# Three conditioning chunks of a two-block transformer kernel computed elsewhere: two in the convolution stage and QKV instead of at the ends of two feed-forward stages

## The reference

```
x = x + rms_norm(mixer(rms_norm(x)))            # block 1: stick-breaking attention, pooling, gating
x = x + rms_norm(relu(h @ w_ff_in)**2 @ w_ff_out)
for i in 0, 1:                                  # block 2: layer 0 conformer convolution, layer 1 attention
    mod = silu(c) @ ada_w[i] + ada_b[i]         # one row of 6 * 1024
    sh1, sc1, g1, sh2, sc2, g2 = split(mod, 6)
    h = rms_norm(x) * (1 + sc1) + sh1
    x = x + g1 * (conv(h) if i == 0 else attention(h))
    h = rms_norm(x) * (1 + sc2) + sh2
    x = x + g2 * (relu(h @ mlp_w1[i])**2 @ mlp_w2[i])
```

## The kernel before, in words

| chunks | where |
|---|---|
| 0, 1 | QKV of block 1 |
| 2, 3 to 8, 9 | first feed-forward stage (`mlp_*` with m = 0): head, loop of three, tail (`ADA_TAIL`) |
| 10 | its end (`ADA_LAST`): first half before the last unit's split, second half after, the sum between the last two units of TensorE, the keeping ahead of what VectorE does to the stage's result |
| 11, 12 | convolution (`ADA_MID`); loaded by GpSimd (`mid_load`, line 854) |
| 13, 14 to 19, 20, 21 | second feed-forward stage (m = 1), as the first |
| 22, 23 | third feed-forward stage (m = 2) |

## Time and profile before

### The profile page before, as it was taken

The page is one execution under the profiler, slowest core; times in us unless marked ns, Lnnn a source line. Parts: engine busy times, 40 slices in busy tenths (PEclk is TensorE's granted clock), DMA queues, the critical chain, the costliest instruction groups (busy, mean ns, idle before and its releaser), DMA issues.

```text
span 1094.3 us, 16806 instructions
## 1 busy us (share of the span) xinstructions
PE 1047.4 (96%) x6872; PEld 922.7 (84%) x6872; DVE 704.1 (64%) x829; ACT 492.0 (45%) x554; POOL 109.7 (10%) x76
## 2 busy tenths in 40 slices
PE   6999998999999999998899999999997799999998
PEld 6997777899999998985689999998886489999996
DVE  4868656687666778653578666687574648454463
ACT  5346446444444445331454443445444844444441
POOL 0030001001001002023101000100000401100000
PEclk9999999899999999998999999999999899999999
DMA  8884435728878783796229787874554224555540
GB/s 291 304 303 132 143 116 159 288 81 310 293 253 290 272 280 105 216 260 197 79 77 345 254 288 265 283 264 145 192 193 133 98 78 154 193 184 199 185 162 39
DMA packets 118716, 221.58 MB, mean 202 GB/s; under 512 B 6338, under 2 KB 20740, under 8 KB 118660
## 3 DMA queue, kind: packets, MB, share of 16 engines
q1 hardware_dynamic: 116944, 214.97, 58.0%
q0 software_dynamic: 1520, 5.77, 1.6%
q10 hardware_dynamic: 196, 0.05, 0.0%
HBM read 215.07 MB, written 1.05 MB: 197 GB/s over the span
## 4 chain that ended last, share of the span: by engine, by line
PE 82%; DVE 8%; ACT 5%; issue 3%; DMA 2%; SPq 1%; ACTq 0%; DVEq 0%
PE ps L410 76%; ACT hi L348 2%; PE ps L870 2%; DVE lo L359 1%; PE ps L447 1%; DVE ada_acc L893 1%; DMA ada_raw<-in_ada_w 1%; PE ps L724 1%; PE ps L650 1%; DVE stat L1914 1%; DMA raw<-in_w_in 0%; DVE hTl L497 0%; ACT aS L1617 0%; DVE aS L1909 0%; ACT gate L1518 0%
## 5 line engine op out<-in xcount | busy, mean ns | idle before, releaser
L359 DVE TENSOR_TENSOR lo<-raw,hi 128x2048 fp32r<-128x2048 f32 x153 | 355.9, 2332 | 277.7 <-ACT hi L348 276.9
L348 ACT ACTIVATE hi<-raw 128x2048 fp32r<-128x2048 f32 x153 | 292.4, 1913 | 332.5 <-PE ps L410 318.8
L410 PE MATMUL ps<-hTh,hi 128*128 128x256 f32 x992 | 282.7, 285 | 2.0 <-DVE hTl L497 1.9
L410 PE MATMUL ps<-hTh,lo 128*128 128x256 f32 x992 | 280.7, 283 | 0.0
L410 PE MATMUL ps<-hTl,hi 128*128 128x256 f32 x992 | 280.6, 283 | 0.0
L410 PEld LDWEIGHTS ps<-hTh,hi 128*128 128x128 f32 x992 | 190.2, 192 | 3.8 <-DVE hTl L497 2.5
L410 PEld LDWEIGHTS ps<-hTl,hi 128*128 128x128 f32 x992 | 190.3, 192 | 0.3
L410 PEld LDWEIGHTS ps<-hTh,lo 128*128 128x128 f32 x992 | 190.3, 192 | 0.0
L410 PE MATMUL ps<-hi,hidh 128*128 128x512 f32 x416 | 162.9, 392 | 0.4 <-DVEq L645 0.4
L410 PE MATMUL ps<-hi,hidl 128*128 128x512 f32 x416 | 162.1, 390 | 0.0
L410 PE MATMUL ps<-lo,hidh 128*128 128x512 f32 x416 | 162.0, 389 | 0.0
(11 more groups left out here) (219 smaller groups left out, 877.6 us busy)
## 6 DMA issues: line engine op xcount, KB each, us to landing
raw<-in_mlp_w SPq DMA_DIRECT2D x64, 1024.0 KB, 5.3
ada_raw<-in_ada_w SPq DMA_DIRECT2D x44, 1024.0 KB, 7.4
raw<-in_w_in SPq DMA_DIRECT2D x21, 1024.0 KB, 7.4
raw<-in_w_ff_in SPq DMA_DIRECT2D x16, 1024.0 KB, 5.3
raw<-in_w_ff_out SPq DMA_DIRECT2D x16, 1024.0 KB, 6.9
raw<-in_attn_w_qkv SPq DMA_DIRECT2D x12, 1024.0 KB, 5.4
raw<-in_conv_w_in SPq DMA_DIRECT2D x8, 1024.0 KB, 6.4
taps<-u_pad SPq DMA_DIRECT2D x64, 71.0 KB, 4.6
```

What stands on the lines that cost most here:

```text
L348: nc.scalar.activation(hi[:, slot], raw[:, slot], ACT.Copy).then_inc(hi_made, 1)
L359: nc.vector.tensor_tensor(lo[:, slot], raw[:, slot], hi[:, slot].bitcast(F32), ALU.subtract).then_inc(lo_made, 1)
L410: return nc.tensor.matmul(o, lhs, rhs, start=start, stop=False, skip_group_check=True)
```

## The change

The chunks 10 and 21 leave the ends of the first and the second feed-forward stage. The columns are dealt out anew: the convolution stage now has three chunks, numbers 10, 11 and 12, which are columns 6, 7 and 8 of layer 1; the head and the tail of the second feed-forward stage take columns 10 and 11 of layer 0 as chunks 13 and 20; chunk 21 is computed in QKV (`ADA_QKV`). There are 24 chunks, as before.

The third chunk of the convolution stage has its own accumulator, in the upper half of `row_b`. GpSimd issues its two loads, the first between `stationaries(3)` and `stationaries(4)`, the second between `stationaries(5)` and `stationaries(6)`. VectorE does its halves after the values k = 1 and k = 3 of the loop that takes the mean off, and TensorE sums it between `conv(3)` and `moments(2)`. Chunk 21 is loaded ahead of the units 106 and 107; VectorE does its halves after `dve_step(105)` and `dve_step(106)`; TensorE sums it after unit 107, waits until it is kept, and then does `gate_row(pe, 1, 0)`.

```diff
@@ -196,7 +196,7 @@
         cshift = row_area("cshift", 4096, [P, SEQ])
         crstd = row_area("crstd", 5120, [P, SEQ])
         dw_sel = ada_area("dw_sel", 8192, [P, 2, TAP_GROUPS, STRIPS, CH])
-        mid_acc = [hid_area("mid_acc0", 8192, [P, 512]), ada_acc]
+        mid_acc = [hid_area("mid_acc0", 8192, [P, 512]), ada_acc, row_area("mid_acc2", 6144, [P, 512])]
 
         Qs = big("Qs", 0, [P, TT, D])
         Ks = big("Ks", 8192, [P, TT, D])
@@ -718,7 +718,7 @@
 
 
         def gate_row(pe, layer, i):
-            pe.wait_ge(ada_kept, (11, 21, 22, 24)[2 * layer + i] + 1)
+            pe.wait_ge(ada_kept, (10, 21, 22, 24)[2 * layer + i] + 1)
             for k in range(KT):
                 m = layer * 48 + (2, 5)[i] * 8 + k
                 last = nc.tensor.matmul(ps[:, 6 + k // 4, (k % 4) * P:(k % 4 + 1) * P],
@@ -774,12 +774,7 @@
             first(7, n, n, 8 * m + 7)
             second(0, n + 2, n + 2, 8 * m + 7,
                    (lambda: ada_sum(pe, ADA_TAIL[m][0]), (lambda: gate_row(pe, m - 1, 1)) if m else None))
-            def last_sum():
-                if m:
-                    pe.wait_ge(row_kept, 2)
-                ada_sum(pe, ADA_LAST[m][0])
-
-            second(1, n + 4, n + 4, 8 * m + 8, (last_sum if m < 2 else None, None), final=True)
+            second(1, n + 4, n + 4, 8 * m + 8, final=True)
 
         def mlp_act(act, m):
             u0 = U_MLP[m]
@@ -829,11 +824,11 @@
 
 
         ADA_IN = [(0, 0, 6), (1, 0, 7)]
-        ADA_MID = [(11, 0, 11), (12, 1, 6)]
-
-        ADA_HEAD = ((2, 0, 8), (13, 1, 7), (22, 1, 10))
-        ADA_TAIL = ((9, 0, 9), (20, 1, 8), (23, 1, 11))
-        ADA_LAST = ((10, 0, 10), (21, 1, 9))
+        ADA_MID = [(10 + q, 1, 6 + q) for q in range(3)]
+        ADA_QKV = (21, 1, 9)
+
+        ADA_HEAD = ((2, 0, 8), (13, 0, 10), (22, 1, 10))
+        ADA_TAIL = ((9, 0, 9), (20, 0, 11), (23, 1, 11))
         MID_FIRST, MID_PAST = ADA_MID[0][0], ADA_MID[0][0] + len(ADA_MID)
         STEPS_BEFORE_MID = 8 + 8 * MID_FIRST
 
@@ -937,17 +932,11 @@
             for j in range(4 if m < 2 else 3):
                 if j < 2:
                     ada_unit(dve, ADA_TAIL[m][0], j, skip(m))
-                if j == 3:
-                    ada_unit(dve, ADA_LAST[m][0], 1, skip(m))
                 dve_step(dve, u0 + 26 + j)
                 if j == 1:
                     lo_of(1, 8 * m + 7)
                 if j == 2:
                     ada_keep(dve, ADA_TAIL[m])
-                    if m < 2:
-                        ada_unit(dve, ADA_LAST[m][0], 0, skip(m))
-            if m < 2:
-                ada_keep(dve, ADA_LAST[m])
 
         def mlp_sp(sp, m, w1, w2, ada_free):
             u0 = U_MLP[m]
@@ -1118,8 +1107,6 @@
             for c in range(4):
                 for h in range(2):
                     cin(c, h)
-                    if c == 1:
-                        ada_load(sp, ADA_LAST[0], h)
             spread(0)
             for c in range(2):
                 cout(c, 0)
@@ -1133,8 +1120,8 @@
                 for h in range(2):
                     load(sp, U_QKV + 2 * c + h,
                          rows3(attn_w_qkv_2[0])[:, 4 * h:4 * h + 4, 512 * c:512 * c + 512])
-                    if c == 1:
-                        ada_load(sp, ADA_LAST[1], h)
+                    if c == 0:
+                        ada_load(sp, ADA_QKV, h)
             square(U_WO, attn_w_o_2[0])
             mlp_sp(sp, 2, mlp_w1_2[1], mlp_w2_2[1], (s_z, AT_HEADS))
             for tt in range(TT):
@@ -1341,6 +1328,7 @@
             moments(1)
             pe.wait_ge(ada_kept, MID_FIRST + 2 + 1)
             conv(3)
+            ada_sum(pe, ADA_MID[2][0], mid_acc[2], 0)
             moments(2)
             moments(3).then_inc(cs_sum, 1)
             stay_warm(18)
@@ -1375,6 +1363,8 @@
 
 
             def first_unit_done():
+                ada_sum(pe, ADA_QKV[0])
+                pe.wait_ge(ada_kept, ADA_QKV[0] + 2)
                 gate_row(pe, 1, 0)
 
             qkv(0)
@@ -1838,6 +1828,9 @@
                         op1=ALU.subtract).then_inc(cs_xc, 1)
                 if k == 1:
                     ada_keep(dve, ADA_MID[1], 7)
+                if k in (1, 3):
+                    mid_unit(dve, 2, k // 2)
+            ada_keep(dve, ADA_MID[2], 0)
             dve.wait_ge(cs_sum, 1)
             nc.vector.tensor_scalar(cvar[:], ps[:, 4, SEQ:2 * SEQ], 1.0 / D, EPS, ALU.mult,
                                     ALU.add).then_inc(var_ok, 1)
@@ -1878,8 +1871,12 @@
             gated_dve(dve, 3, U_MLP[1] + 31, row_b)
             mod_hT(5, 6, 1, 0, U_MLP[1] + 31)
             for c in range(6):
+                if c == 1:
+                    ada_keep(dve, ADA_QKV)
                 for h in range(2):
                     dve_step(dve, U_QKV + 2 * c + h)
+                    if c == 0:
+                        ada_unit(dve, ADA_QKV[0], h, skip(1))
                 if c < 4:
                     dve.wait_ge(qk_sq, c + 1)
                     nc.vector.tensor_reduce(stat[:, 64 + 16 * c:80 + 16 * c].rearrange("p (t h) -> p t h", t=TT),
@@ -1987,8 +1984,12 @@
             stationaries(2)
             stationaries(3)
             mid_load(pool, 1, 1)
-            for k in range(4, KT):
-                stationaries(k)
+            mid_load(pool, 2, 0)
+            stationaries(4)
+            stationaries(5)
+            mid_load(pool, 2, 1)
+            stationaries(6)
+            stationaries(7)
 
             pool.wait_ge(row_kept, 1)
             pool.wait_ge(row_c_in, 16)
```

## The result

The changed kernel takes 1103.76 us, the median of 7 runs (1099.54 to 1104.84), against 1096.88 us before (7 runs, 1096.14 to 1097.05): the medians differ by 6.9 us. The ratio of the runs is 1.0056, 95% interval 1.0040 to 1.0072, which is 4.4 to 7.9 us. The forecast was +6.0 us and 1102.8.

A forecast was written before the change was run, and what follows sets the result against it. TensorE, busy for 96% of the span, was taken to bound the kernel, so only its waits counted. The terms -1.5 + 4.7 - 0.8 + 3.6 = +6.0 us took 1096.14 to 1102.1, median 1102.8; range 1096 to 1107.

The forecast's parts named there:

- End of the first feed-forward stage: There, without the chunk, VectorE's third product starts at 417.85 instead of 419.37: -1.5 us.
- Convolution stage: There the second chunk's stall goes, but the third chunk's loads and steps delay the layer norm to 532.2 from 527.5: +4.7 us.
- The removed stall: Convolution stage: TensorE's 3.46 us stall for the second chunk goes, with its 3.0 us of half clock.
- the two waits for the port: Convolution stage, third chunk's second half: VectorE's steps wait for GpSimd's additions until 518.7, then until 521.6.
- a sign of being wrong: Convolution stage: loads landing in less than 6.5 us, or TensorE never idle before the third sum, would refute the forecast.
- End of the second feed-forward stage: There TensorE has no sum of 0.81 us and the end follows TensorE: -0.8 us.
- QKV: There TensorE waits for chunk 21's steps and sum, so the gate row begins at 784.75 against 781.14: +3.6 us.
- rival 1: QKV: the clock falls there too, price 3.0 us, total 1105.8 us; chance 0.13.
- Rival 2: Convolution stage: the clock stays up, moments take 3.76 us, the part is +1.3, total 1099.4 us; chance 0.12.
- Rival 3: Convolution stage: GpSimd's last three operations don't delay VectorE; TensorE waits 2 us, clock stays, total 1096.6 us; chance 0.12.
- Rival 4: Convolution stage: loads quick, port waits stay, VectorE ends near 520; sum -1.3, total 1095.5 us; chance 0.05.
- Rival 5: Convolution stage: bound by TensorE, the new chunk hides; part -5.3, sum -4.0, total 1092.8 us; chance 0.11.

The follow-up runs named there:

- the convolution half: The changed kernel with chunk 21 back at the end of the second feed-forward stage: 1099.04 us, ratio 1.0027 to the kernel before.
- the QKV half: The kernel before with chunk 21 alone moved from the end of the second feed-forward stage to QKV: 1100.57 us, ratio 1.0034.
- loads held: The changed kernel with SyncE's loads for the next feed-forward stage held back until both halves of the third chunk have landed: 1102.00 us, ratio 1.0055.
- the second trace of the kernel after: The changed kernel unaltered, measured again beside the kernel before on the chip of other runs: 1101.86 us, ratio 1.0050.
- the kernel before with its port free: The kernel before with one wait more: GpSimd makes `dw_sel` 4 and later only after VectorE's last step of the second chunk: 1092.62 us, ratio 0.9969.
- the idle products: The changed kernel with 20 idle products on TensorE, results unused, ahead of the third chunk's sum: 1102.25 us, ratio 1.0047.
- rows after: The changed kernel with GpSimd's product of rows and two additions to `x` held until the third chunk's steps are done: 1102.25 us, ratio 1.0057.
- the kernel with both: The changed kernel with SyncE's next loads held back and GpSimd's row work behind the third chunk: 1096.71 us, ratio 1.0002.
- sum late: The changed kernel with chunk 21 summed between units 109 and 110 and the gate row no longer waiting for it: 1101.95 us, ratio 1.0043.
- two and two: The changed kernel with two convolution chunks, chunks 20 and 21 in QKV, and `dw_sel` 4 after the second chunk's last step: 1095.22 us, ratio 0.9989.

## Why the prediction was right, point by point

The forecast held in sign and size, and the waits that it named are those of the trace. That it came so near, +6.0 against +6.9, is in part luck: its four terms came to less than it said, and falls of the clock that it had left out made up for them. By the medians of the two parts run alone, the convolution half cost 2.6 us where -1.5 + 4.7 = 3.2 was forecast, and the QKV half 4.2 where -0.8 + 3.6 = 2.8 was. The steps can be compared with those of the trace, once the shift of what lies ahead is taken off.

- **End of the first feed-forward stage**: -1.5 predicted, -1.65 measured. The square comes when ScalarE is free, the third product right behind it. TensorE's idle products end 0.96 us earlier, not 0.8, and of its wait 1.25 + 0.96 - 1.64 = 0.57 us is left, near the 2.05 - 1.5 = 0.55 of the forecast. GpSimd's earlier `dw_sel` did hold VectorE up (a subtraction took 2.93 us and a split 4.00, instead of 1.21 and 2.29), but the stretch of -1.65 shows nothing of that.
- **Convolution stage**: +4.7 predicted, +3.97 measured. The removed stall and the second chunk came as forecast: the sum 2.66 us earlier than 498.4, which is the shift. The third chunk was forecast to be done at 523.7; it was done at 520.24 + 2.66 = 522.9, and TensorE idled 4.77 us against 4.7. Two terms were mis-sized in opposite ways, the loads: 6.4 and 10.4 us instead of 7.9 and 8.6, in sum 16.8 and 16.5. GpSimd's additions ended at 517.33 + 2.66 = 520.0, not 521.1, and the second half landed at 515.99 + 2.66 = 518.65, not 518, so it met one of the two waits for the port that were forecast. Its steps took 4.25 us, not over 5; with the loads held they met three operations of GpSimd and took 8.30. The first load, at 6.4 us, was also under the 6.5 that the prediction had named as a sign of being wrong; the second, at 10.4, kept the sum of the two where it was. That the shared ports are held for a whole operation and not divided, as the Trainium skill has it (SBUF — State Buffer, SBUF: two separate sides), agrees with both numbers. The sum and the moments took 528.81 - 520.29 = 8.5 us against 1.2 + 7.2 = 8.4, but only in this execution: in the second trace of the kernel after they took 7.0, because the clock came back sooner, and C is 2.3 us over before there, half of the forecast.
- **End of the second feed-forward stage**: -0.8 predicted, -0.97 measured.
- **QKV**: +3.6 predicted. The gate row starts 24.90 us after the diagonals (761.87 to 786.77) instead of 21.40 (759.74 to 781.14): +3.50. The wait for the keeping is 0.35, where 784.75 - 784.5 = 0.25 was allowed, and the sum took 1.05 rather than 1.2. Behind the gate row stand one unit and four pairs, not the six pairs of the prediction; nothing hangs on that.
- **Left out of the sum**: the clock in QKV (that was rival 1), in the output product and in the attention. The four terms make -1.65 + 3.97 - 0.97 + 3.50 = +4.85. The rest of this execution's 8.9 lies where the clock is at half: in the output product (+1.79), in the gate row and behind it (4.48 - 3.50 + 0.70 = +1.68), in the transposes of Q (+1.57), less the 1.01 ahead of the change. The last one isn't the change's own: the kernel before with its port free has 79.48 there too, with a fall at the same place. By the medians, +6.9, some of this isn't there; the second trace of the kernel after has V at 39.99 and A at 76.91. So rival 1 came true in part: the clock did fall in QKV, for 1.7 us rather than 3.0, and with a shorter idling than the 4.6 us that I set against it.
- **Rival 2** (the clock stays up in the convolution stage) is what the idle products made: C fell by 2.2 to 3.9 us, forecast 7.2 - 3.76 = 3.4, but the time didn't follow. **Rival 3** is the kernel with the rows after: the steps took 3.1 as it said, but the load's 10.2 us kept the wait at 3.43, not 2, and the clock fell. **Rival 4** is the kernel with the loads held: the landing was quick, the port waits were there, and the third chunk was done at 511.66 + 8.30 = 519.96, which is 522.0 in the times of the trace before, not near 520: the port held the steps for three operations; TensorE idled 3.87 and the clock fell, which the rival had left out. **Rival 5** needed both; its C of -5.3 is 93.02, the kernel with both had 93.90.

Of the four repairs made singly (sum late, loads held, rows after, idle products) none made the change neutral; rivals 3 and 4 each took away one cause and left the other standing.

## What to carry to other kernels

Where two causes would each hold an instruction until about the same moment, mending one is worth next to nothing: price the pair, and try the pair. Before work is moved into a stage, look at what its new load or wait orders on an engine that shares a port: that order alone, put into the kernel before as one wait, was worth 3.7 us, while the move as made cost 6.9. A sum over a chunk that nothing needs yet belongs well behind the last step that it waits for: one unit behind it TensorE waited 1.92 us, here and in the version with two and two, and a pair of units later than that not at all.

## What the runs showed of the hardware

- A load issued by GpSimd takes 6.4 us and 10.4 us in the same kernel, issued 9.6 us apart; the longer one shares the DMA engines with SyncE's loads (share 1.06 at 508:510), and with these held back it takes 5.4 to 5.5.
- Operations of VectorE with two inputs in SBUF wait for operations of GpSimd's to end, and with work queued on both they took turns here: the pair on line 1832 took 2.47 us instead of 0.75, and four steps beside three operations of GpSimd's 8.30 instead of 3.11.
- TensorE's granted clock falls to 0.50 (1.2 GHz) in different places in executions of the same kernel (at 832 to 836 in one trace of the kernel after, not there in the other), and keeping it up at 518 won nothing in the whole that could be measured. The kernel after took 1099.54 to 1101.85 us in executions with a mean clock of 0.989, and 1104.43 to 1104.98 in those with 0.982. What decides it stays open.
